# Layer attention of a transformer kernel in 16 rounds of four units in place of 32 steps of two, on one Trainium2 core

## The reference, cut to what matters

```python
for l in range(DEPTH):                       # DEPTH = 2
    h = _rmsnorm(x, norm_g[l]); p = _split(h @ w_in[l])
    o_a = _mla(...)        # A: 4 heads, low-rank q and kv, softmax(q k) v
    o_b = _diff_attn(...)  # B: 4 heads with two maps each: a = p[0] - lam * p[1]; o = a v
    o_c = _dsa(...)        # C: 4 heads over the 128 keys that an index picks per query
    o_d = _short_conv(...)
    y = concatenate([o * silu(gate) for each of the four])
    x = x + y @ w_out[l]
```

## Time and profile before

| | us |
|---|---|
| median of 3 runs (lowest, highest) | 1785.37 (1785.29, 1786.74) |
| the profiled execution's span | 1785.4 |
| TensorE busy | 1776.4 (99%) |
| VectorE busy | 1062.3 (59%) |
| ScalarE busy | 750.5 (42%) |
| GpSimd busy | 407.3 (23%) |

### The profile page before, as it was taken

The page is one execution under the profiler, slowest core; times in us unless marked ns, Lnnn a source line. Parts: engine busy times, 40 slices in busy tenths (PEclk is TensorE's granted clock), DMA queues, the critical chain, the costliest instruction groups (busy, mean ns, idle before and its releaser), DMA issues.

```text
span 1785.4 us, 25187 instructions
## 1 busy us (share of the span) xinstructions
PE 1776.4 (99%) x9274; PEld 1437.2 (80%) x9274; DVE 1062.3 (59%) x2106; ACT 750.5 (42%) x1386; POOL 407.3 (23%) x248
## 2 busy tenths in 40 slices
PE   9999999999999999999999999999999999999998
PEld 7767778776777888888888878879888888888887
DVE  5888777588877665445433445555756654555333
ACT  6464654446454533223222455545444322232222
POOL 4544553455354310000000232220200200000000
PEclk9999999999999999999999999999999999999999
DMA  5422222322212343333333422323321333333332
GB/s 188 125 81 70 60 59 85 97 81 83 67 53 60 96 138 102 95 94 94 106 106 104 150 60 83 95 72 107 95 73 55 92 101 94 94 94 101 99 106 94
DMA packets 49765, 165.53 MB, mean 93 GB/s; under 512 B 5640, under 2 KB 6152, under 8 KB 49672
## 3 DMA queue, kind: packets, MB, share of 16 engines
q1 hardware_dynamic: 48376, 161.47, 30.2%
q10 hardware_dynamic: 1296, 2.84, 0.4%
HBM read 162.12 MB, written 2.17 MB: 92 GB/s over the span
## 4 chain that ended last, share of the span: by engine, by line
PE 97%; DVE 1%; ACT 1%; issue 0%; POOL 0%; DVEq 0%; POOLq 0%
PE proj L1013 78%; PE turned L1302 2%; PE o L1326 2%; PE score L1276 2%; PE turned L1530 1%; PE proj L1460 1%; PE o L1556 1%; PE score L1521 1%; PE proj L1453 1%; PE score L1285 1%; PE o L1652 1%; PE turned L979 1%; PE score L1641 1%; PE score L1163 0%; PE proj L991 0%; PE turned L998 0%
## 5 line engine op out<-in xcount | busy, mean ns | idle before, releaser
L1013 PE MATMUL proj<-hhi,whi 128*128 128x512 f32 x1456 | 580.2, 399 | 0.6 <-DVE tanh L2285 0.3
L1013 PE MATMUL proj<-hhi,wlo 128*128 128x512 f32 x1456 | 568.1, 390 | 0.0
L1013 PE MATMUL proj<-hlo,whi 128*128 128x512 f32 x1456 | 567.3, 390 | 0.0
L1736 ACT ACTIVATE whi<-ring 128x1024 fp32r<-128x1024 f32 x279 | 295.2, 1058 | 622.7 <-PE proj L1013 614.4
L2201 DVE TENSOR_TENSOR wlo<-ring,whi 128x1024 fp32r<-128x1024 f32 x199 | 243.1, 1222 | 164.8 <-ACT whi L1736 164.5
L1013 PEld LDWEIGHTS proj<-hhi,whi 128*128 128x128 f32 x1456 | 274.3, 188 | 59.4 <-issue 6.6
L1013 PEld LDWEIGHTS proj<-hhi,wlo 128*128 128x128 f32 x1456 | 273.4, 188 | 58.8
L1013 PEld LDWEIGHTS proj<-hlo,whi 128*128 128x128 f32 x1456 | 274.0, 188 | 52.8
L759 POOL TENSOR_TENSOR wlo<-ring,whi 128x1024 fp32r<-128x1024 f32 x80 | 194.7, 2435 | 372.6 <-ACT whi L1736 372.0
L771 POOL TENSOR_TENSOR prob<-prob 128x512 f32<-128x512 f32 x36 | 56.6, 1574 | 873.9 <-ACT prob L1732 873.9
L1762 ACT ACTIVATE prob<-prob,negmax 128x256 f32<-128x256 f32 (+3 forms) x208 | 114.4, 552 | 65.5 <-DVE negmax L2274 64.1
(11 more groups left out here) (334 smaller groups left out, 2426.1 us busy)
## 6 DMA issues: line engine op xcount, KB each, us to landing
ring<-wstream SPq DMA_DIRECT2D x287, 512.0 KB, 3.6
arena<-lines SPq DMA_DIRECT2D x28, 256.0 KB, 5.5
arena<-x ACTq DMA_DIRECT2D x4, 512.0 KB, 5.9
out<-arena SPq DMA_DIRECT2D x8, 256.0 KB, 2.9
arena<-mem SPq DMA_DIRECT2D x1, 1024.0 KB, 9.4
ring<-wstream ACTq DMA_DIRECT2D x2, 256.0 KB, 7.3
arena<-hot SPq DMA_DIRECT2D x2, 80.0 KB
par<-params ACTq DMA_DIRECT2D x2, 74.0 KB, 1.9
```

Of the source, the lines that this page charges most:

```text
L1013: mm = pe.matmul(b, rounded(w), rounded(rhs(v, k)), start=(first and n == 0 and p == 0), stop=(last and n == len(blocks) - 1 and p == 2))
L1736: act.activation(rounded(dst), src, ACT.Copy, scale=scale).then_inc(ready, 1)
```

## The change

The 32 steps become 16 rounds of four units, that is of two steps. In B a round takes both heads and both maps of a query block, on four row groups at once. The four units have the four banks `score[0]`, `score[1]`, `turned[0]`, `turned[1]`, into which the round's probabilities are also turned afterwards. In C a round is two pairs one after the other, in A four single units; there a round has the query blocks 0 and 3, or 1 and 2.

TensorE's order in round t is `turn(t-1)`, the fillers of slot 2t, `pv(t-1)`, `scores(t)`, the fillers of slot 2t+1. `scores(0)` now waits for `latent_ready`, and `scores(t)` for the copies of all turned groups of the round before. The planner gives each even slot 2.4 us of fillers and shares the rest among the odd ones; worked out, the even slots get four chunks as a rule, the odd ones 6 to 11 fillers. In round 0 these are BQ1's chunks 0 to 3; BQ1's chunks 4 to 7, VN0 and BK1's chunks 0 and 1.

VectorE's order in round t: low halves of y, gates, the top-k halves of slot 2t, convolution, the evictions of slot 2t; `row_mins(t)` for four units; early evictions of slot 2t+1; `row_scales` for both steps; then the same side work of slot 2t+1 with its top-k halves. So the two halves of slot 0, which stood behind the first minima, now stand ahead of them. ScalarE's: copies of the groups of round t-1; the work after slot 2t; four exponentials; the work after slot 2t+1, which includes the rounding of an evicted BQ1 in round 0.

The diff's core (the gates, convolutions and copies are the same calls in new places):

```diff
-def attention_cost(s):
...
+def round_need(t):
+    if t == ROUNDS:
+        return 4.5
+    return 3.8 + 0.85 * step_qb(2 * t) if 2 * t < B_STEPS else 5.5
...
-            pieces.append((name, 0, {"UQ": 2.9, "UK": 1.5, "UV": 1.5, "VN": 0.5, "SS": 1.0, "SR": 1.0}[name[:2]]))
+            pieces.append((name, 0, {"UQ": 2.0, "UK": 1.0, "UV": 1.1, "VN": 0.45, "SS": 1.7, "SR": 1.6}[name[:2]]))
...
+        t = s // 2
+        if s % 2 == 0:
+            room = FIRST_PART
+        else:
+            left = sum(p[2] for p in pieces[at:]) - FIRST_PART * (ROUNDS - t)
+            room = left * round_need(t) / sum(round_need(u) for u in range(t, ROUNDS + 1))
...
-O_STEP = (10, 18, 22, 26, 32, 34)
+O_ROUND = (4, 8, 10, 12, 14, 16)
+O_STEP = tuple(2 * t + 1 for t in O_ROUND)
...
+        four_banks = (score[0], score[1], turned[0], turned[1])
...
-                def scores(s):
-                    if s == 0:
+                def scores(t):
+                    if t == 0:
                         pe.wait_ge(relu_ready, L * IDX_UNITS + IDX_UNITS)
+                        pe.wait_ge(latent_ready, L * 3 + 3)
                         pe.wait_ge(b_ready, L * 4 + 2)
                     else:
-                        pe.wait_ge(min_ready, L * LAYER_SM + 2 * s)
+                        pe.wait_ge(min_ready, L * LAYER_SM + 4 * t)
+                        pe.wait_ge(turn_out, L * LAYER_GR + groups_before(2 * t))
...
+                    elif branch == "B":
+                        for p, (q_part, k_part) in enumerate(((bq_hi, bk_hi), (bq_hi, bk_lo), (bq_lo, bk_hi))):
+                            for u in range(4):
+                                part(u, q_part, k_part, p == 0, p == 2)
                     else:
...
+                        for i in range(2):
+                            for p, (q_part, k_part) in enumerate(((cq_hi, ck_hi), (cq_hi, ck_lo), (cq_lo, ck_hi))):
+                                for h in range(2):
+                                    part(2 * i + h, q_part, k_part, p == 0, p == 2)
...
-                for s in range(FILL_STEPS + 1):
-                    if s < STEPS:
-                        scores(s)
-                    if s >= 3:
-                        pv(s - 3)
-                    if 2 <= s < FILL_STEPS:
-                        turn(s - 2)
-                    for name, k in PLAN[s] if s < FILL_STEPS else ():
+                for t in range(ROUNDS + 1):
+                    if t == 0:
+                        scores(0)
+                    else:
+                        turn(t - 1)
+                    for name, k in PLAN[2 * t]:
+                        fill(name, k)
+                    if t > 0:
+                        pv(t - 1)
+                        if t < ROUNDS:
+                            scores(t)
+                    for name, k in PLAN[2 * t + 1]:
                         fill(name, k)
...
+                for t in range(LAST_STEP // 2):
+                    if 0 < t <= ROUNDS:
+                        copy_groups(t - 1)
+                    gates_of(2 * t - 1)
+                    after_slot(2 * t)
+                    diags_of(2 * t)
+                    y_highs(2 * t)
+                    if t < ROUNDS:
+                        for u in range(4):
+                            a = 4 * t + u
+                            s = a // 2
+                            softmax_exp(L * LAYER_SM + (a + 1), u, width(step_qb(s)),
+                                        first_sum(s) if s < B_STEPS and u % 2 == 0 else None)
+                    gates_of(2 * t)
...
+                    diags_of(2 * t + 1)
+                    after_slot(2 * t + 1)
+                    y_highs(2 * t + 1)
...
+                for t in range(LAST_STEP // 2 + 1):
+                    a, b = 2 * t, 2 * t + 1
+                    y_lows(a)
+                    gates_of(a - 2)
+                    topk_of(a)
+                    convs_of(a - 1)
+                    for name in ENDED[a] if t <= ROUNDS else ():
+                        evict(name)
+                    if t < ROUNDS:
+                        row_mins(t)
+                    if t in O_ROUND[:2]:
+                        o_out(O_ROUND.index(t))
+                    for name in EARLY[b] if t <= ROUNDS else ():
+                        evict(name)
+                    if t < ROUNDS:
+                        row_scales(a)
+                        row_scales(b)
+                    y_lows(b)
+                    gates_of(b - 2)
+                    if t in O_ROUND[2:]:
+                        o_out(O_ROUND.index(t))
+                    topk_of(b)
+                    convs_of(b - 1)
+                    for name in ENDED[b] if t <= ROUNDS else ():
+                        if name not in EARLY[b]:
                             evict(name)
```

More of the change, by code:

```diff
@@ L217 @@
 FILL_STEPS = STEPS + 2
+ROUNDS = STEPS // 2
 QB_ORDER = (0, 3, 1, 2)
+FIRST_PART = 2.4
 def step_qb(s):
@@ L1266, in scores, with part @@
                         pe.wait_ge(up_out, L * 4 + 2)
-                    if s == C_STEP:
+                    if 2 * t == C_STEP:
                         pe.wait_ge(c_ready, L * 4 + 2)
-                    if s == C_STEP + 4:
+                    if 2 * t == C_STEP + 4:
                         pe.wait_ge(c_ready, L * 4 + 4)
-                    def parts(b, q_part, k_part, first, last):
-                        branch, pair, qb, h, m = UNITS[2 * s + b]
+                    def part(u, q_part, k_part, first, last):
+                        branch, pair, qb, h, m = UNITS[4 * t + u]
                         q, W = slice(qb * P, (qb + 1) * P), width(qb)
                         rows = slice(HD * h + 32 * m, HD * h + 32 * m + 32) if branch == "B" else slice(HD * h, HD * h + HD)
-                        mm = pe.matmul(score[b][:, 0:W], rounded(q_part[rows, pair, q]), rounded(k_part[rows, pair, 0:W]),
+                        mm = pe.matmul(four_banks[u][:, 0:W], rounded(q_part[rows, pair, q]), rounded(k_part[rows, pair, 0:W]),
                                        start=first, stop=last)
@@ L1279, in parts @@
                             mm.then_inc(score_done, 1)
-                    branch, pair, qb = UNITS[2 * s][:3]
+                    branch = UNITS[4 * t][0]
                     if branch == "A":
-                        for b in range(2):
-                            hh, q, W = 2 * pair + b, slice(qb * P, (qb + 1) * P), width(qb)
-                            pe.matmul(score[b][:, 0:W], qA[0:96, hh, q], kA[0:96, hh, 0:W], start=True, stop=True).then_inc(score_done, 1)
-                    else:
-                        (q_hi, q_lo), (k_hi, k_lo) = ((bq_hi, bq_lo), (bk_hi, bk_lo)) if branch == "B" else ((cq_hi, cq_lo), (ck_hi, ck_lo))
-                        for p, (q_part, k_part) in enumerate(((q_hi, k_hi), (q_hi, k_lo), (q_lo, k_hi))):
-                            for b in range(2):
-                                parts(b, q_part, k_part, p == 0, p == 2)
@@ new lines, in turn @@
+                def turn(t):
+                    for s in (2 * t, 2 * t + 1):
+                        pe.wait_ge(scaled_ready, L * LAYER_SM + (2 * s + 2))
+                        for n, g in enumerate(step_groups(s)):
+                            for kb in range(step_qb(s) + 1):
+                                mm = pe.transpose(four_banks[g % 4][:, kb * P:(kb + 1) * P],
+                                                  prob[:, (2 * s + n) % 4, kb * P:(kb + 1) * P], ident[:, :])
+                            mm.then_inc(turn_done, 1)
@@ L1314, in pv @@
+                def pv(t):
+                    branch, pair = UNITS[4 * t][:2]
+                    o = step_groups(2 * t)[0] // 8
+                    if groups_before(2 * t) % 8 == 0:
                         if o >= 2:
```

187 lines of the change are left out of this document (78 added, 109 removed).

## The result

The changed kernel takes 1806.62 us (median of 4 runs, 1803.5 to 1809.48), the kernel before beside it 1785.33 (1785.01 to 1786.74): a ratio of 1.0115, 95% interval [1.0102, 1.0128]. It is slower by about 21 us where 12 us less was forecast. The four runs lie in two groups, two near 1804 with a granted clock of 0.998 and two near 1809 with 0.995; the profiled one is of the first group (1804.29 us, span 1802.5).

The account below looks back on a forecast made before the run. TensorE was taken as the bound, 97% of the last chain. 1785.4 less 21.2 saved (Parts 1 and 2) plus 9.0 of new waits (Parts 3 and 4) gave 1773.2 us; forecast 1770 to 1778, range 1765 to 1788.

Parts of the forecast that it names:

- Part 1: B's scores on TensorE: a quad on four row groups costs as much as one pair, saving 5.5 us a layer.
- Part 2: TensorE's attention order: fewer changes between kinds of matmul, beyond B's pairs, save 5.1 us a layer.
- Part 3: Attention start: TensorE waits before first scores, transposes and PV: 0.95, 2.2, 0.8 us in first layer; 0.95, 0.3, 0.8 in second.
- Part 4: Later rounds: late scalings make TensorE wait 1.2 us a layer in B, 0.3 in round 12; bounds 0 and 6.
- Rival 4: VectorE becomes the bound of B's, then A's rounds; 1802 us, or 1789 with 0.6 us lost a round; chance 0.14.
- Rival 3: B's quads run in two turns and save nothing: 1784.2 us; chance 0.14 together with another rival.

Follow-up runs that it names:

- fifth kernel: Changed kernel with VectorE's scalings ahead of the early evictions and two of GpSimd's four rotations of A's queries moved to slots 12 and 14; 1785.21 us.
- experiments 2 and 9: On the changed kernel: 2 held GpSimd's odd-slot low halves until the round's scalings were done, 1793.41 us; 9 moved A's and C's scalings to ScalarE, 1803.82 us.
- eleventh kernel: Fifth kernel with round 0's top-k halves behind scalings and BQ1's and VN0's evictions, and ScalarE's rounding after UQ2 behind round 2's group copies; 1777.39 us.
- experiment 3: Changed kernel with B's four units listed as two pairs in turn, all six matmuls of the first pair ahead of the second's; 1810.59 us.
- experiment 4: Changed kernel with the two top-k halves of slot 0 put back behind the first four minima, still ahead of the scalings; 1809.53 us.
- experiment 6: Fifth kernel with the top-k halves of slot 0 put behind the first scalings of the attention; 1785.91 us.

## Why the prediction was wrong, point by point

- **Part 1** (5.5 us a layer from the quads) was right: 5.3.
- **Part 2** (5.1 us a layer from fewer changes of kind) was right in kind and too high by 1.0: 18.7 - 10.6 = 8.1 us in both layers. The scores of A and C gave 2.4 a layer where 1.1 was taken, the PV runs 1.1 for 1.4. The transposes gave nothing where 2.4 was taken: I had costed a run of them like a run of PV, with a start of 0.15 beyond its matmuls. But 120 of them take 12.50 us in 32 runs in the second layer of the kernel before (13.27 in the first, where a run of eight at 209.02 fell to the lower clock) and 13.21 in 16 runs in the fifth kernel, 0.10 to 0.11 each; a run of them has no start to save.
- **Part 3, first layer** was right in place and size: 0.91 us before the scores (0.95 forecast), 1.48 + 0.58 before the transposes (2.2), 0.69 before the first PV (0.8). **Second layer**: 0.90, 2.15 and nothing, where 0.95, 0.3 and 0.8 were forecast. The first minimum did come early against the scores, as I had taken it (398.37 for scores at 393.4, against 82.22 for 74.97 in the first layer: 2.3 us). What failed is the price of the joins: 1.02 us was taken for the whole work of a step's scaling, and the two joins alone took 1.18 and 1.92, beside a rotation and a low half of GpSimd. It is the step that failed in part 4, met here first.
- **Part 4 is the step that failed: the duration of the joins and scalings, and the slack that they had.** I took 1.5 us a layer with bounds of 0 and 6, and it was 15.0 - 3.7 = 11.3 in the first and 14.0 - 3.1 = 10.9 in the second. The margin of 0.8 us in a round of width 512 was worked out with the joins at their mean duration, and the scalings of A and C were given no window at all. The row that speaks of it stood in front of me, L2460 with 1198 ns in the earlier trace rows and "no row here tells what stretches them". GpSimd's rows in the same stretch would have told: its low half runs beside the long ones. Two terms were missing: the early eviction waits for a job's end and holds the scalings (1.72 us at 246.55), which I had only for rounds 6 and 7, and that same end starts the low half that then holds them again (3.69 for 0.75). By experiments 2 and 9, which leave the eviction ahead, the second is the one that made A's and C's transposes wait. A third, smaller one stood nowhere: a low half itself comes late behind GpSimd's rotations, 1.64 us in each layer.
- **Nothing was set for the clock.** 11 more half-speed distances cost 2.2 us in the profiled run, and the two runs near 1809 have a lower clock still. 0.003 of the clock over 1805 us is 5.4 us, an estimate, and they are 5 us longer.
- **The rivals.** Rival 4 was nearest in time (1789 to 1802) and named the right waits, transposes late for the scalings in most rounds; its reason, VectorE full, was wrong. VectorE was idle for 15 of the 90 us of B's rounds. It wasn't short of time but held up. The Trainium skill's rule that I cited for it (TensorEngine Tiling (Array Packing), section "PSUM Bottleneck") doesn't decide here either: in the list of TensorE's waits no minimum stands, though the minima are what empties the banks, and the eleventh kernel is faster with the same minima. Rival 3 fell with the quads.
- **The sum with what was measured**: 1785.4 - 18.7 + 29.2 + 3.0 + 3.6 = 1802.5. With most of part 4's waits gone, the eleventh kernel's span is 1775.6, 2.4 us over the forecast. So the change carries most of the gain that the forecast saw, once four places in the other engines' lists are put right. Whether such moves would have helped the kernel before wasn't run, but it had only 2.0 us of idle time to win.

## What to carry to other kernels

When the steps of a pipeline are made coarser, price the critical engine's saving, and then list for each other engine what stands ahead of the last instruction that it waits for, and what the same trigger starts elsewhere. An instruction whose mean is twice its best at equal shape may be in a clash that had cover until now, as it was here: look up what ran beside it before the cover is removed. And put the instruction that the bound engine waits for ahead of any that waits for the bound engine.

## What the runs showed of the hardware that I had not expected

- By the records, matmuls on other row groups start past those queued ahead of them (if the chip ran the list as written): with the six matmuls of one pair first in the list, the other pair's first one starts 0.02 us after the first and not 0.6 us later (experiment 3).
- The lower clock mostly follows stands of 1.6 to 3.9 us (or two closer together, such as 1.23 and 0.60), with projections at 0.427 us apart for 2 to 5 us; in the kernel before at 208.8 us it follows none. The kernels with the longest stands aren't those with the most such distances: experiment 4 has 25, experiment 6 has 7. What else decides is open.
- Two VectorE scalings of 384 columns beside GpSimd's low half and addition took 3.69 us for 0.75, each ending 0.2 us after the GpSimd instruction beside it. Of two joins of width 128 one took 1.92 us beside a low half, 0.35 without.
